# Where the adaLN modulation rows of a two-layer diffusion block are computed, and in which shape

## The reference, cut to what matters

```
mod = silu(cond) @ w_ada + b_ada          # cond: 2 rows (latent, context) x 1024, w_ada: 1024 x 6144
shift1, scale1, gate1, shift2, scale2, gate2 = split(mod, 6)
h   = rms_norm(x, g) * (1 + scale) + shift
x   = x + gate * mixer(h)
```

## Time and profile before

| | us |
|---|---|
| time of the two runs | 4974.92 and 4975.96, median 4975.44 |
| span of the profiled execution (first to last instruction) | 4976.5 |
| start of the first w_ada product (line 227) | 23.39 |
| start of the first w_in product (line 427) | 145.76 |
| first product of the scan to its last DVE addition | 534.19 to 771.23 |
| both PEER stages together, product line 1542 busy | 2396.5 |

### The profile page before, as it was taken

How to read it: one execution, slowest core, us unless ns; L and a number is a source line. 1 busy time by engine, 2 the same in 40 slices (tenths; PEclk the granted TensorE clock), 3 DMA queues, 4 the chain that set the end, 5 groups by cost and what they waited for, 6 DMA issues and landing times. The chain is left out here.

```text
span 4976.5 us, 44098 instructions
## 1 busy us (share of the span) xinstructions
PE 4056.6 (82%) x12322; PEld 2081.6 (42%) x12322; DVE 3019.9 (61%) x7079; ACT 1093.1 (22%) x2793; POOL 1564.2 (31%) x1382
## 2 busy tenths in 40 slices
PE   7899897867878787878787877789777788778877
PEld 1555794433434343433333333368333333333333
DVE  0340453267777777777777773654267777777776
ACT  0110221122222222222222222245122222222221
POOL 0000220034444444444444440000044444444442
PEclk9999898988989998999999998899888899999898
DMA  6110232089999999999999992000199999999997
GB/s 234 68 51 23 86 108 71 18 363 417 403 414 399 416 399 413 404 411 400 408 405 413 405 414 90 38 1 1 62 398 419 417 412 408 404 407 414 401 402 325
DMA packets 288367, 1460.76 MB, mean 294 GB/s; under 512 B 24576, under 2 KB 95936, under 8 KB 124096
## 3 DMA queue, kind: packets, MB, share of 16 engines
q0 software_dynamic: 184320, 1342.26, 65.6%
q1 hardware_dynamic: 103872, 116.62, 7.0%
HBM read 1456.66 MB, written 2.13 MB: 293 GB/s over the span
## 5 line engine op out<-in xcount | busy, mean ns | idle before, releaser
L1542 PE MATMUL banks<-arena 128*128 128x512 f32 x5120 | 2396.5, 626 | 679.5 <-ACT arena L1577 679.1
L1474 POOL DMA_INDIRECT arena<-experts,arena x1280 | 1491.7, 1165 | 2673.1 <-PE banks L1542 1356.7
L1663 DVE CUSTOM_DVE_ANT_0 arena<-arena 128x1024 f32<-128x1024 f32 x1280 | 1536.7, 1224 | 776.8 <-DMA arena<-experts,arena 693.2
L1542 PEld LDWEIGHTS banks<-arena 128*128 128x128 f32 x5120 | 1014.4, 201 | 2020.0 <-issue 1226.8
L1577 ACT ACTIVATE arena<-arena 128x128 f32<-128x128 f32 x1280 | 407.7, 389 | 451.5 <-DVE arena L1670 438.6
L1570 ACT ACTIVATE arena<-arena 128x4 f32<-128x4 f32 x320 | 66.0, 206 | 1683.9 <-DVE arena L1663 1683.9
L1488 PE MATMUL banks<-arena 128*128 128x512 f32 (+1 forms) x864 | 329.5, 529 | 16.7 <-DMA arena<-wq 16.7
L1488 PEld LDWEIGHTS banks<-arena 128*128 128x128 f32 x864 | 165.4, 193 | 176.3 <-issue 144.1
L427 PE MATMUL banks<-arena 128*128 128x512 f32 (+1 forms) x640 | 210.5, 489 | 10.1 <-DMA arena<-l_w_in 10.1
L738 POOL TENSOR_TENSOR arena<-arena 128x256 f32<-128x256 f32 x48 | 30.4, 633 | 549.1 <-ACT arena L641 385.6
L922 PE MATMUL banks<-arena 128*128 128x512 f32 x416 | 184.4, 607 | 14.8 <-DMA arena<-l_w_out 8.3
(11 more groups left out here) (199 smaller groups left out, 3525.2 us busy)
## 6 DMA issues: line engine op xcount, KB each, us to landing
arena<-l_w_ada SPq DMA_DIRECT2D x12, 2048.0 KB, 7.9
arena<-l_w_ada SPq DMA_DIRECT2D x24, 1024.0 KB, 5.2
arena<-experts,arena POOLq DMA_INDIRECT x1280, 17.3
arena<-wq SPq DMA_DIRECT2D x36, 512.0 KB, 23.9
arena<-l_w_in SPq DMA_DIRECT2D x7, 2048.0 KB, 7.8
arena<-l_w_out SPq DMA_DIRECT2D x4, 1536.0 KB, 12.2
arena<-l_w_o SPq DMA_DIRECT2D x4, 1024.0 KB, 8.5
arena<-gates SPq DMA_DIRECT2D x7, 512.0 KB, 12.5
```

What stands on the lines that cost most here:

```text
L1474: pool.indirect_dma_start(slots[s], None, tbl, bass.IndirectOffsetOnAxis(ap=expert[:, t % 2, k:k + 1], axis=0)).then_inc(land[s]["sem"], 16)
L1542: mm = pe.matmul(core["ps"][:, 2 * (t % 2) + c, :], diag[:, k % (2 * BATCH), :], v[:, D + c * 512:D + (c + 1) * 512], start=(k == 0), stop ...
L1663: dve.tensor_tensor_reduce(u, u, h2[:, t, :], 1.0, 0.0, ALU.mult, ALU.add, dots[:, k:k + 1]).then_inc(dot["sem"], 1)
```

## The change

`load_constants`, `ada_stage` and the first `norm_stage` become one `front_stage`. It computes only the first third of layer 0's modulation (shift1 and scale1, 2048 columns). `w_ada` comes in eight loads of 128 x 2048 (1 MB, rows of 8 KB) into eight places of their own, on SP's queue, followed there by the first two chunks of `w_in`; x, context and constants come on ACT's queue. The condition is padded with zeros to 32 columns, and each slice is multiplied in four products: product j streams columns 512 j to 512 j + 511 into PSUM partitions 32 j to 32 j + 31 of one bank. Squares, row scaling and the turning of the first two tiles do not wait for the modulation. One DVE addition takes the bank out with the bias, four turns of 128 x 128 make columns.

The other five thirds (two of layer 0, three of layer 1) are computed in the scan: five groups of nine steps, in which the first eight steps take one slice each and the ninth turns the rows; the last three steps take none. SP loads 40 slices through two slots and stores gate rows directly from the row form. Gates are stored and loaded as whole rows of 1024 words. The projection no longer issues its first two loads.

```
+def ada_slice(pe, core, wt, k, bank):
+    cond = view(core, COND_O, KD, 32)
+    for j in range(4):
+        i = pe.matmul(core["ps"][32 * j:32 * j + 32, bank, :], cond[:, k, :], wt[:, j * 512:(j + 1) * 512],
+                      start=(k == 0), stop=(k == KD - 1))
+    return i
+def ada_turn(pe, core, row, bank):
+    for b in range(4):
+        i = pe.transpose(core["ps"][:, bank, b * P:(b + 1) * P], row[:, b * P:(b + 1) * P], ident(core))
+    return i
...
+def front_stage(core, d):
...
+            sp.dma_start(cond, d["cond"]).then_inc(cl["sem"], up(cl, 16))
+            for k in range(KD):
+                sp.dma_start(slices[k], d["l0_w_ada"][k * P:(k + 1) * P, 0:GP]).then_inc(ws[k]["sem"], up(ws[k], 16))
+            for c in range(2):
+                sp.dma_start(view(core, RO + c * SLOT, KD, 512),
+                             w_in[:, :, W_IN_STARTS[c]:W_IN_STARTS[c] + 512]).then_inc(wf[c]["sem"], up(wf[c], 16))
...
+            for k in range(KD):
+                pe.wait_ge(ws[k]["sem"], at(ws[k], 16))
+                i = ada_slice(pe, core, slices[k], k, 4)
+            i.then_inc(mm["sem"], up(mm))
+            pe.wait_ge(const["sem"], at(const, 64))
+            turn(0)
+            turn(1)
+            pe.wait_ge(ro["sem"], at(ro, 1))
+            ada_turn(pe, core, row, 5).then_inc(tc["sem"], up(tc))
+            for t in range(2, TT):
+                turn(t)
...
+    groups = [(0, 1), (0, 2), (1, 0), (1, 1), (1, 2)]
...
+                    if q * KD + k >= 2:
+                        sp.wait_ge(am["sem"], at(am, q * KD + k - 1))
+                    sp.dma_start(ada_w[s], d[f"l{layer}_w_ada"][k * P:(k + 1) * P, g * GP:(g + 1) * GP]
+                                 ).then_inc(sig["sem"], up(sig, 16))
...
+                q, k = divmod(n, KD + 1)
+                if q < len(groups) and k == KD - 1:
+                    dve.wait_ge(bl[q % 2]["sem"], at(bl[q % 2], 16 * (q // 2 + 1)))
+                    dve.wait_ge(am["sem"], at(am, (q + 1) * KD))
...
+                    dve.tensor_tensor(ada_row, core["ps"][:, 7, :], ada_bias[:, q % 2, :],
+                                      ALU.add).then_inc(ar["sem"], up(ar))
+                if q < len(groups) and k == KD:
+                    dve.wait_ge(atr["sem"], at(atr, q + 1))
+                    ada_columns(dve, core, *groups[q], 7, ao)
...
-                i = ada_tile(pe, core, ada_w[s], n % 2, n, 7)
-                if n % 2:
-                    i.then_inc(am["sem"], up(am))
+                if q < len(groups) and k < KD:
+                    s, sig, v = plan[q * KD + k]
+                    if k == 0 and q:
+                        pe.wait_ge(ao["sem"], at(ao, cols[q]))
+                    pe.wait_ge(sig["sem"], v)
+                    ada_slice(pe, core, ada_w[s], k, 7).then_inc(am["sem"], up(am))
+                if q < len(groups) and k == KD:
+                    pe.wait_ge(ar["sem"], at(ar, q + 1))
+                    ada_turn(pe, core, ada_row, 7).then_inc(atr["sem"], up(atr))
```

More of the change, by code:

```diff
@@ L59 @@
 WORDS = 53208
+COND_O = MISC + 1536
+GP = 4 * 512
 def up(sig, n=1):
@@ new lines, with ada_columns @@
+SCALES = {0: (1, 0), 2: (4, 1)}
+def ada_columns(dve, core, layer, g, bank, done):
+    mod = view(core, S_MOD + layer * 96, 6 * KD, 2)
+    norms = view(core, S_NORM + layer * 2 * KD, 2, KD)
+    turned = core["ps"][:, bank, :].rearrange("p (b j m) -> p j b m", b=4, j=4)[:, :, :, 0:2]
+    dve.tensor_copy(mod[:, g * 2 * KD:(g + 1) * 2 * KD, :].rearrange("p (j b) m -> p j b m", b=4),
+                    turned).then_inc(done["sem"], up(done))
+    if g in SCALES:
+        part, n = SCALES[g]
+        c2 = mod[:, part * KD:(part + 1) * KD, :]
+        dve.wait_ge(done["sem"], done["total"])
+        dve.scalar_tensor_tensor(out=c2, in0=c2, scalar=1.0, in1=bcast(norms[:, n, :], 2),
+                                 op0=ALU.add, op1=ALU.mult).then_inc(done["sem"], up(done))
@@ L128, in load_constants, with gate_rows @@
+def gate_rows(core, layer, kind, cond):
+    return core["gates"][layer, kind, cond:cond + 1, :].to_broadcast([P, D])
+def front_stage(core, d):
     nc = core["nc"]
-    loaded = signal(core, "constants_loaded")
-    silu_done = signal(core, "cond_silu_done")
     cond = view(core, S_COND, KD, 2)
+    cond32 = view(core, COND_O, KD, 32)
+    bias = view(core, L0 + 8 * GP, 512)
+    row = view(core, L0 + 8 * GP + 512, 512)
+    x = view(core, XO, TT, D)
+    ht = view(core, HO, KD, TOK)
+    squares = view(core, L0 + 8 * GP + 1024, D)
+    xn = view(core, L0 + 8 * GP + 2048, 2, D)
+    slices = [view(core, L0 + k * GP, GP) for k in range(KD)]
+    ss = view(core, MISC, TT)
+    rstd = view(core, MISC + 8, TT)
+    mod = view(core, S_MOD, 6, 2 * KD)
+    shift, scale = (mod[:, n, :].rearrange("p (k c) -> p k c", c=2) for n in range(2))
+    w_in = d["l0_w_in"].rearrange("(k p) n -> p k n", p=P)
+    cl = signal(core, "condition_loaded")
+    const = signal(core, "constants_loaded")
+    xl = [signal(core, n) for n in ("latents_loaded", "context_loaded")]
+    ws = [signal(core, f"ada_slice{k}_loaded") for k in range(KD)]
+    wf = [signal(core, f"w_in_first{c}_loaded") for c in range(2)]
+    zero = signal(core, "condition_zeroed")
+    silu = signal(core, "condition_silu_done")
+    mm = signal(core, "ada_product_done")
+    ro = signal(core, "ada_rows_out")
+    tc = signal(core, "ada_rows_turned")
+    cm = signal(core, "ada_columns_ready")
+    sq = signal(core, "norm_squares_summed")
+    root = signal(core, "norm_root_done")
+    own = signal(core, "norm_rows_ready")
+    tr = signal(core, "norm_rows_turned")
+    cola = signal(core, "norm_low_columns_out")
+    colv = signal(core, "norm_high_columns_out")
@@ L146, in _ @@
+        @block.gpsimd
+        def _(pool):
+            pool.memset(view(core, COND_O, KD * 32), 0.0).then_inc(zero["sem"], up(zero))
         @block.scalar
         def _(act):
[L148 to L159, removed]
@@ L162, in ada_columns @@
[L162 to L173, removed]
@@ L176, in ada_turn_gates @@
[L176 to L217, removed]
@@ new lines, in _ @@
+            act.dma_start(bias, d["ada_rows"][0]).then_inc(const["sem"], up(const, 16))
+            act.dma_start(view(core, S_BF, 192), d["const_bf"]).then_inc(const["sem"], up(const, 16))
+            act.wait_ge(cl["sem"], at(cl, 16))
+            act.wait_ge(zero["sem"], at(zero, 1))
+            act.activation(cond32[:, :, 0:2], cond, ACT.Silu).then_inc(silu["sem"], up(silu))
+            for t in range(TT):
+                if t in (0, TL):
+                    act.wait_ge(xl[t // TL]["sem"], at(xl[t // TL], 16))
+                if t:
+                    act.wait_ge(sq["sem"], sq["total"])
+                act.activation(squares, x[:, t, :], ACT.Square,
+                               accum_out=ss[:, t:t + 1]).then_inc(sq["sem"], up(sq))
@@ new lines, in _ @@
+            act.wait_ge(own["sem"], at(own, 1))
+            act.activation(rstd, ss, ACT.Sqrt).then_inc(root["sem"], up(root))
+            act.wait_ge(cm["sem"], at(cm, 2))
+            for t in range(TT):
+                c = 0 if t < TL else 1
+                act.wait_ge(tr["sem"], at(tr, t + 1))
+                for k in range(KD // 2):
+                    i = act.activation(ht[:, k, t * P:(t + 1) * P],
+                                       pair(core, 2 * (t % 2))[:, k * P:(k + 1) * P], ACT.Identity,
+                                       bias=shift[:, k, c:c + 1], scale=scale[:, k, c:c + 1])
+                i.then_inc(cola["sem"], up(cola))
@@ new lines, in _, with rows @@
+        @block.vector
+        def _(dve):
+            def rows(t):
+                if t >= 2:
+                    dve.wait_ge(tr["sem"], at(tr, t - 1))
+                dve.tensor_scalar(xn[:, t % 2, :], x[:, t, :], rstd[:, t:t + 1], None,
+                                  ALU.mult).then_inc(own["sem"], up(own))
+            dve.wait_ge(sq["sem"], at(sq, TT))
+            dve.tensor_scalar(ss, ss, 1.0 / D, EPS, ALU.mult, ALU.add).then_inc(own["sem"], up(own))
+            dve.wait_ge(root["sem"], at(root, 1))
+            dve.reciprocal(rstd, rstd).then_inc(own["sem"], up(own))
+            dve.wait_ge(own["sem"], own["total"])
+            rows(0)
+            rows(1)
+            dve.wait_ge(const["sem"], at(const, 64))
+            dve.wait_ge(mm["sem"], at(mm, 1))
+            dve.tensor_tensor(row, core["ps"][:, 4, :], bias, ALU.add).then_inc(ro["sem"], up(ro))
+            dve.wait_ge(tc["sem"], at(tc, 1))
+            ada_columns(dve, core, 0, 0, 5, cm)
+            dve.wait_ge(cm["sem"], at(cm, 2))
+            for t in range(TT):
+                c = 0 if t < TL else 1
+                dve.wait_ge(tr["sem"], at(tr, t + 1))
+                for k in range(KD // 2, KD):
+                    i = dve.tensor_scalar(ht[:, k, t * P:(t + 1) * P],
+                                          pair(core, 2 * (t % 2))[:, k * P:(k + 1) * P],
```

(43 more changed lines are left out.)

86 lines of the change are left out of this document (38 added, 48 removed).

## The result

The changed kernel takes 4838.38 us (median of 4838.35 and 4838.40) against 4975.44: ratio 0.972, 95% interval 0.970 to 0.975, so 2.8% faster. The forecast was 4890; the time lies in the range (4825 to 4954), at the rival *side by side* (4835). The range is 129 us wide and was made to hold three cases; of the outcomes, faster by over 2% had been given 0.32 and a change within 2% 0.64, so the less likely one came. By spans the change is 4836.5 - 4976.5 = -140.0 us.

A forecast was written before the change was run, and what follows sets the result against it. PE's list was taken to bound the scan, a serial chain the 145.76 us before the projection. 4976.5 - 91.3 (front) + 5.5 (scan) = 4890.7, less 1.1 to the runs' median: 4890, range 4825 to 4954.

The forecast's parts named there:

- side by side: Rival, scan and front: all four strips of a slice run at once, 0.88 + 0.1 us; total 4835, chance 0.29.
- three cases: Strips all at once, overlapping in pairs, or queueing: 4835, 4890, 4945; none under 2 in 10, so the range holds them.
- the front: Stretch before the projection: starts at 54.4 in place of 145.76, bounded by loads, 91.3 us less.
- price of a slice: Scan: four products of a slice take 5 x 0.438 = 2.19 us, plus 0.1 a step for switching.
- list order: Main case for slices: records start in the code's order, so strips overlap in pairs; total 4890, chance 0.35.
- five row turns: Scan: five turns of 8 records, 0.12 us each, 4.9 us added in all.
- if strips overlap otherwise than in pairs: Sign for the slices' products that would show the forecast of 4890 wrong.
- change of shape: Scan: switching between strips and whole array, twice a step; taken as 0.1 us a step, at most two operand loads of 0.12.
- The stage's end: End of the scan stage: loses columns, turn of gates and store, 3.3 us, of which 0.3 stay; 3.0 less.
- SP's waits: Scan: SP waits for a group's row before storing gates, 3 us once a group, against a step of 5.3.
- One after the other: Rival: strips queue like any products, 3.50 + 0.1 us a slice; scan +59.2, total 4945, chance 0.28.
- Low clock: Rival, scan: strips queue and the granted clock falls to 1.2 GHz; about 5199 us, chance 0.04.

The follow-up runs named there:

- in one strip: Changed kernel with all products of the front's slices 1 to 7 put into strip 0, scan left as it was: 4847.86 us, ratio 0.974.
- whole-array kernel: Changed kernel whose scan slices have one 512-column product with the unit matrix over the whole array, replacing four products in strips: 4825.24 us, ratio 0.970.
- pairs of steps: Changed kernel doing two steps' slices at one visit every second step, with only every second slice loaded and used twice: 4831.24 us, ratio 0.971.
- two-strip kernels: Changed kernel with a scan slice's four products put into strips 0, 0, 1, 1 or 0, 1, 0, 1: 4872.58 and 4875.17 us.
- early turns: Changed kernel with the turns of the first two tiles moved ahead of the front's slices 5 and 6: 4845.82 us, ratio 0.972.

## Why the prediction was right or wrong

**Right: the direction, and the front.** 94.5 us less against 91.3 forecast. Its terms one by one: the last slice at 33.65 (34 forecast), its products 1.94 (2.2; that they agree is luck, two records a strip at half the rate against five at the full one), two turns 3.68 (3.67), the row turn 0.78 (1.8: four records, not the eight that I counted), tiles 10.6 (11.2). That the loads bound it is shown by the wait for a load ahead of every slice; in one strip, at 3.79 a slice, PE bounds it instead.

**Wrong: the price of a slice.** The step that failed is "a product's second record needs the strip that its first one occupies, so if records start in list order, the second record of strip j runs beside the first of strip j+1, and a slice takes 5 x 0.438 = 2.19". The premise about list order fell: each strip works off its own records, whatever stands ahead of them in the list. The earlier trace rows could not show it, since only products over the whole array occur there: "nothing there shows one overtaking another" was read as evidence, and was none. Above the prediction's 2.99 a slice costs 0.88 in records and 0.41 beside them, 1.29 in place of 2.29: 41 us of the scan, which came out at -35.3 where I had +8.5. The other 2.7 are the five row turns: four records, not eight, and 0.44 us each, 2.2 in place of 4.9. By its own sign ("if strips overlap otherwise than in pairs") the forecast of 4890 was wrong.

**Wrong in size: the change of shape.** Taken at 0.1, bounded at 0.24; it is 0.31 by the whole-array kernel, and 0.34 by pairs of steps ((2 x 4.28 - 8.22) a visit saved). The bound had two operand loads, but PE also stops bringing loads forward for 0.84 us after the strips. In the case side by side, whose scan was put at -45.2 and came out at -35.3, 8.6 us are this (41 x 0.21) and 4.1 the plain step (3.09 in place of 2.99); the row turns give 2.7 back.

**Right: what costs nothing.** The stage's end gave 3.0 as forecast, the gates' rows in the out stages nothing. SP's waits behind the new order stay off the path (one of those for a group's row lasted 10.0, where 3 was put); in the answer on SP's waits, to be set beside the earlier trace rows:

```profile
SPq L699 <- PE banks L132: 178.9, 38, 27.4
SPq L688 <- DVE arena L810: 14.3, 4, 10.0
```

**Left out:** scatter behind the scan of some 7 us between executions of the same code, which at 4890 or 4835 would have been a term of the range. That 4838 came so near the 4835 of *side by side* is luck for that reason: against its terms the scan is 9.9 us worse, the front 2.0 better, and 7.2 better are stretches that the sum put at nothing.

**The rivals.** *One after the other* and *list order* are both refuted by the two-strip kernels; one after the other does give what it was priced at when it is made (6.84 a step, 6.6 forecast). *Low clock*: the scan's granted clock is 0.98, near the full 2.4 GHz.

## What to carry to other kernels

Products that hold 32 columns ran side by side in strips here, and only the strip with the longest chain cost time, in either order of the list that was tried. Each visit to strips between products over the whole array costs about 0.3 us here, so gather the strip work of several steps at one visit and pay with a slot of memory. Before a step is moved ahead, look up every load that it waits for: the queue of the constants, not the engine, decided the early turns.

## What the runs showed of the hardware that was not expected

In the front a slice takes 1.94 us and in the scan 1.06, and yet the clock column reads 1.00, the full 2.4 GHz, from 9.0 to 35.6. That 1.00 is no reading: the trace of the changed kernel holds no record of the granted clock before 39.34 us, and the view counts a stretch without one as 1.00. The scan's first slice, 3.7 us after PE had idled for 6.5, has a record at the lower level (0.50, which is 1.2 GHz), and it takes the same 1.94:

```profile
438.84 1.97 PE L871 MATMUL banks<-arena 128*128 128x64 f32 x8 [6.51 <-DVE arena L776]
...
442.55 1.94 PE L132 MATMUL banks<-arena 128*32 128x512 f32 x8
```
```profile
442.50:444.40 1.90, 1.90 (x9) 0.20 (x8) 1.71 (x4) 0.00 (x0) 1.44 (x2) 0.50 0.00 0
```

With all products of the front in one strip, PE does not idle between slices. The first 3.8 us there hold 5 records and the next 3.8 hold 9, in the same column at 1.00:

```profile
13.70:17.50 3.80, 3.78 (x5) 0.89 (x6) 0.00 (x0) 3.71 (x7) 0.00 (x0) 1.00 1.02 425
17.50:21.30 3.80, 3.80 (x9) 0.91 (x8) 0.00 (x0) 1.28 (x3) 0.00 (x0) 1.00 1.01 417
```

That trace's first record of the clock, at the full level, begins at 18.44, where the distance of two records falls from 0.85 to 0.43 us. In the kernel before it is 26.61, and line 227 goes from 0.85 to 0.43 a record there; so its 84.14 us hold some slow records, and a price taken from a stretch ahead of the first record of the clock is no price for a busy engine. By the rates, the changed kernel's slices in front ran at the lower level; no record says so directly. For the first seven slices this changed nothing, because the loads came slower still. Behind the last one it cost time: two turns took 3.68 us, and 1.97 with the front in one strip.
